# Mixer: the second rotation and the scan's input in PSUM in place of V, two scans of 264

## The chip, the cores and the metric

The kernel runs on one core of a Trainium2 chip. The metric is the device time of one execution in microseconds; lower is better. The core has five engines that run side by side and meet by semaphores: TensorE (PE, matrix products and transposes, its weight loads shown as PEld), VectorE (DVE), ScalarE (ACT), GpSimd (POOL) and SyncE (SP, which issues DMAs here). PE writes to PSUM, an accumulator memory of eight banks; DVE and ACT read and write both PSUM and SBUF, POOL works in SBUF alone.

## What is computed

A decoder trunk of two layers on 528 tokens (16 meta tokens and 512 of the input) with 1024 channels, all in float32. Layer 0 mixes tokens with a diagonal state-space model (S5), layer 1 with differential attention; each is followed by a gated conv-FFN. The change lies in the S5 mixer:

```python
def s5_mixer(u, a_re, a_im, log_dt, b_re, b_im, c_re, c_im, d_skip, w_glu, b_glu):
    """u: (B, L, D). Groups of 16 channels drive a 64-dim complex diagonal state (MIMO)."""
    ...
    ug = u.astype(f32).reshape(bsz, L, S5_GROUPS, S5_GROUP)
    bu_re = jnp.einsum('blgc,gnc->blgn', ug, bb_re)
    bu_im = jnp.einsum('blgc,gnc->blgn', ug, bb_im)
    a_seq_re = jnp.broadcast_to(ab_re, (1, L, S5_GROUPS, S5_STATE))
    a_seq_im = jnp.broadcast_to(ab_im, (1, L, S5_GROUPS, S5_STATE))
    _, _, s_re, s_im = lax.associative_scan(
        _complex_linear_combine, (a_seq_re, a_seq_im, bu_re, bu_im), axis=1)
    y = (jnp.einsum('blgn,gcn->blgc', s_re, c_re.astype(f32))
         - jnp.einsum('blgn,gcn->blgc', s_im, c_im.astype(f32)))
    y = y.reshape(bsz, L, D_MODEL) + d_skip.astype(f32) * u.astype(f32)
    z = jax.nn.gelu(y).astype(u.dtype)
    h = z @ w_glu + b_glu
    val, gate = jnp.split(h, 2, axis=-1)
    return val * jax.nn.sigmoid(gate)
...
    for i in range(DEPTH):
        j = i // N_MIXERS
        hn = rms_norm(h, norm_mix_gain[i])
        if i % N_MIXERS == 0:
            mix = s5_mixer(hn, ...)
        else:
            mix = diff_attention(hn, ...)
        h = h + mix.astype(h.dtype)
        hn = rms_norm(h, norm_ffn_gain[i])
        h = h + conv_ffn(hn, ffn_w_up[i], ffn_conv_w[i], ffn_conv_b[i], ffn_w_down[i]).astype(h.dtype)
```

The state of a group is a complex recurrence s(t) = a s(t-1) + B u(t) along the tokens, for 64 groups of 64 states.

## The kernel before

**Stages.** A prologue computes powers of a and the tables; the S5 loop runs over eight blocks of 128 channels (CT = 8, b = 0 to 7); then come the GLU (16 units of weights), the FFN of layer 0, attention with its output projection, and the FFN of layer 1. From the GLU on, weights are loaded, split into a high and a low part by ACT and POOL, and multiplied by PE.

**The S5 loop.** The 528 tokens are taken as NK = 66 chunks of T = 8. Within a chunk the outputs come from a direct product (TT, Toeplitz), between chunks from a state that is carried 66 times. Per block there are eight groups (BG), so real and imaginary part of four pairs (BQ) times 66 chunks make 2 x 264 = 528 columns on 128 partitions. PE's `inject(b)` (L708) writes these injections, V, to PSUM banks 2 and 3. A complex recurrence with a fixed rotation is turned into a real one: DVE's `scan(b)` multiplies V by the tables T1 and T2 of cosines and sines (L1650, L1651: "rotations", to rt1 and rt2), combines the products into zin (L1654, L1655: "sums"), shifted by one chunk, and runs one `tensor_tensor_scan` over 528 columns with the decay R (L1657) into zst. R is zero at the first chunk of each row, which restarts the scan. `states(b)` turns the result back (L1662, L1663), sums it to Sst (L1668, L1669), and PE multiplies it with E.

**The order of the work.** All orders are written out by hand, one instruction stream for each engine, with semaphores between them. In turn b of its loop

- DVE does `scan(b)`, `states(b)`, then for the next block E (`output_product`, `output_powers`, L1578 and L1594) and the tables T (`rotation_products`, `rotation_sums`, L1624 to L1633), and `z_rest(b - 1)` (L1676), the low part of the GLU's input.
- PE does `inject(b)`, transposes of x (L650), of z (L746) and of the scaled input (L662), then `input_weights(b + 1)` (L673, L675: transposes of F1 and F2 into PSUM banks 2 and 3), `state_outputs(b)` (L727, after DVE's Sst), `direct_outputs(b)` (L735, after the DMAs of TT) and `kernel_products(b + 1)` (L692, L697, after E). In turn 7 it has six tiles of GLU unit 0 (L769) in place of the input weights.
- ACT copies between PSUM and SBUF: among others `weights_out` (L1230, WBT, from the transposes), the first power of F (`unscaled_weights`, L1191), `decay` (R, L1251), `gelu` (L1268), `mirror` (L1258, the other half of the tables), `kernel_out` (L1240).
- POOL computes F1 and F2 of the next block (`input_power`, L525), four multiplications. It starts when DVE has finished that block's tables (`t_set`) and PE the last transposes (`ft_ps`). After the last tables it splits the weights of GLU unit 0 (L301).
- SP issues the DMAs of the inputs and, after `kernel_out`, the sixteen of TT by halves of the loop; then the GLU's weights.

`input_weights(b + 1)` may write banks 2 and 3 when V has been read: it waits for `v_read`, which the two rotations raise. GLU unit 1, which uses the same banks, waits for the same semaphore (L759).

## Time and profile before

| | us |
|---|---|
| median of three runs | 1314.66 |
| lowest and highest | 1309.7, 1315.55 |
| the profiled execution, device time | 1313.71 |
| its span in the profile | 1311.9 |
| mean granted clock of PE in it | 0.984 of full |

The profile gives for each engine the time in which it was busy, the idle time before an instruction and what ended it, and the chain of waits: the work that ended last, followed back to what released it. Times in the rows are us from the start of the span. PE and PEld overlap. "1.00" and "0.50" are the two levels of PE's granted clock, 2.4 and 1.2 GHz; a stretch that has both shows a mean between them.

### The profile page before, as it was taken

Reading aid. Unit: us, or ns where it says so; the run is one execution under the profiler, and the core shown is the slowest. Engines: PE = TensorE matmul, PEld = TensorE weight load, DVE = VectorE, ACT = ScalarE, POOL = GpSimd, SP = SyncE. Lnnn points to the kernel's source line nnn. Section 1 sums busy time; section 2 is a strip of 40 time slices with the busy share of each in tenths; the row PEclk is TensorE's granted clock in tenths of the full one; section 3 lists DMA queues with packets and bytes.
Section 4 is the critical chain, followed back from the end, with each engine's and each line's share of the span. In section 5 each row is a group of like instructions: output and inputs, shape, how many; then the busy total and the mean of one; then the engine's idle time right before and its main releaser. Section 6 shows DMA issues by size and latency. Waiting matters only on the chain.

```text
span 1311.9 us, 26207 instructions
## 1 busy us (share of the span) xinstructions
PE 1252.9 (96%) x10291; PEld 1192.5 (91%) x10291; DVE 764.3 (58%) x1027; ACT 566.0 (43%) x951; POOL 603.1 (46%) x365
## 2 busy tenths in 40 slices
PE   4787999999999999999999999989999999999998
PEld 4676899999999999999988889979999999997886
DVE  6699522388888886111345555553488888882002
ACT  6867443433334343222556665633334343432113
POOL 5223376543444435665644545407644444344441
PEclk9689999999999999999999999999999999999999
DMA  9222342233332232333221211212332323332221
GB/s 168 48 61 51 88 113 85 66 91 96 96 96 80 82 94 88 101 88 108 69 79 49 64 51 49 65 32 66 97 96 85 93 79 95 96 96 96 97 94 67
DMA packets 179546, 108.88 MB, mean 83 GB/s; under 512 B 7164, under 2 KB 173837, under 8 KB 179213
## 3 DMA queue, kind: packets, MB, share of 16 engines
q1 hardware_dynamic: 178885, 107.29, 29.2%
q8 instruction: 51, 0.84, 0.3%
q10 hardware_dynamic: 592, 0.60, 0.2%
q14 instruction: 18, 0.15, 0.0%
HBM read 101.58 MB, written 2.10 MB: 79 GB/s over the span
## 4 chain that ended last, share of the span: by engine, by line
PE 35%; issue 31%; DVE 14%; POOL 14%; ACT 4%; DMA 1%; DVEq 1%; POOLq 0%; ACTq 0%; SPq 0%
PE ps L877 9%; POOL wL L301 9%; PE ps L926 9%; PE ps L769 7%; DVE cv L1735 4%; DVE cv L1741 2%; PE ps L963 2%; PE ps L1033 1%; POOL acc L1960 1%; POOL sqt L1959 1%; DVE cg L1748 1%; DVE u L1730 1%; DVE u L1731 1%; PE ps L314 1%; ACT actH L1348 1%
## 5 line engine op out<-in xcount | busy, mean ns | idle before, releaser
L301 POOL TENSOR_TENSOR wL<-raw,wH 128x1024 fp32r<-128x1024 f32 x182 | 445.2, 2457 | 556.8 <-ACT wH L297 540.6
L297 ACT ACTIVATE wH<-raw 128x1024 fp32r<-128x1024 f32 x182 | 186.4, 1048 | 238.8 <-PE ps L314 82.9
L314 PE MATMUL ps<-hgH,wH 128*128 128x264 f32 (+1 forms) x1408 | 285.5, 284 | 2.7 <-DVE hgL L1698 2.7
L314 PE MATMUL ps<-hgH,wL 128*128 128x264 f32 (+1 forms) x1408 | 285.3, 284 | 0.0
L314 PE MATMUL ps<-hgL,wH 128*128 128x264 f32 (+1 forms) x1408 | 285.1, 284 | 0.0
L314 PEld LDWEIGHTS ps<-hgH,wH 128*128 128x128 f32 x1408 | 218.9, 189 | 3.2 <-issue 3.0
L314 PEld LDWEIGHTS ps<-hgL,wH 128*128 128x128 f32 x1408 | 218.4, 189 | 0.0
L314 PEld LDWEIGHTS ps<-hgH,wL 128*128 128x128 f32 x1408 | 217.8, 189 | 0.0
L1346 ACT ACTIVATE cg<-cg 128x528 f32<-128x528 f32 (+1 forms) x44 | 28.2, 640 | 268.2 <-DVE cg L1741 268.2
L1735 DVE TENSOR_SCALAR cv<-u,PV 128x528 f32<-128x528 f32 (+1 forms) x44 | 111.3, 2529 | 0.0
L1741 DVE SCALAR_TENSOR_TENSOR cg<-u,PV,cg 128x528 f32<-128x528 f32 (+1 forms) x88 | 97.3, 1105 | 13.0 <-DVE cv L1735 6.7
L926 PE MATMUL ps<-hgH,wH 128*128 128x264 f32 x384 | 83.7, 299 | 0.0
L926 PE MATMUL ps<-hgH,wL 128*128 128x264 f32 x384 | 78.6, 286 | 0.0
L926 PE MATMUL ps<-hgL,wH 128*128 128x264 f32 x384 | 78.4, 286 | 0.0
L314 PE MATMUL ps<-actH,wH 128*128 128x264 f32 x352 | 71.2, 283 | 0.0
L314 PE MATMUL ps<-actH,wL 128*128 128x264 f32 x352 | 71.2, 283 | 0.0
L314 PE MATMUL ps<-actL,wH 128*128 128x264 f32 x352 | 71.2, 283 | 0.0
L1741 DVE SCALAR_TENSOR_TENSOR cv<-u,PV,cv 128x528 f32<-128x528 f32 (+1 forms) x88 | 66.2, 752 | 0.0
L1409 ACT ACTIVATE Pb<-ps,tiny 128x144 f32<-128x144 f32 (+4 forms) x66 | 34.7, 531 | 69.3 <-DVE tiny L1789 69.2
L1763 DVE TENSOR_TENSOR ytok<-ps,fgain 128x512 f32<-128x512 f32 x4 | 2.8, 692 | 105.8 <-ACT ysq L1365 105.8
L926 PEld LDWEIGHTS ps<-hgH,wH 128*128 128x128 f32 x384 | 59.8, 191 | 3.9 <-issue 3.8
L1735 DVE TENSOR_SCALAR cg<-u,PV 128x528 f32<-128x528 f32 (+1 forms) x44 | 55.7, 1267 | 8.5 <-DVE u L1731 8.5
(299 smaller groups left out, 2375.0 us busy)
## 6 DMA issues: line engine op xcount, KB each, us to landing
raw<-ffn_w_up SPq DMA_DIRECT2D x88, 512.0 KB, 3.8
raw<-ffn_w_down SPq DMA_DIRECT2D x38, 512.0 KB, 3.5
raw<-attn_w_qkv SPq DMA_DIRECT2D x24, 512.0 KB, 3.7
raw<-s_w_glu SPq DMA_DIRECT2D x16, 512.0 KB, 4.0
TT<-KD SPq DMA_DIRECT2D x64, 64.0 KB, 2.4
raw<-attn_w_o SPq DMA_DIRECT2D x8, 512.0 KB, 4.1
raw<-ffn_w_down SPq DMA_DIRECT2D x8, 384.0 KB, 3.4
xb<-x SPq DMA_DIRECT2D x8, 256.0 KB
```

The lines of the kernel that those rows point to most:

```text
L297: nc.scalar.activation(wH[:, slot, 0:nk], raw[:, slot % 2, 0:nk], ACT.Copy).then_inc(w_hi, 1)
L301: nc.gpsimd.tensor_tensor(wL[:, slot, 0:nk], raw[:, slot % 2, 0:nk], wH[:, slot, 0:nk].bitcast(F32), ALU.subtract).then_inc(w_lo, 1)
L314: mm = nc.tensor.matmul(ps[:, bank + b, 0:tw], w[:, slot, k, :], x[:, kt, t0:t0 + tw], start=first and k == 0 and s0, stop=last and k == n ...
L769: mm = nc.tensor.matmul(ps[:, bank + b, 0:tw], w[:, n % 4, k, :], x[:, k, t0:t0 + tw], start=k == 0 and s0, stop=k == 7 and s1)
L877: mm = nc.tensor.matmul(ps[:, 2 * t + c, :], x[:, kt, tok], w[:, n % 4, 4 * c:4 * c + 4], start=False, stop=last and w is ws[-1] and x is ...
L926: mm = nc.tensor.matmul(ps[:, unit_bank(n) + b, 0:tw], w[:, n % 4, k, :], x[:, k, t0:t0 + tw], start=k == 0 and s0, stop=k == 7 and s1)
L963: return nc.tensor.matmul(ps_row[:, base[c] + a:base[c] + b], q[half[c], q0:nk], k[half[c], a:b], start=True, stop=stop)
L1033: mm = nc.tensor.matmul(out_at(i), AT[:, t, :], values, start=t == 0, stop=t == n_tiles(i) - 1)
L1346: nc.scalar.activation(cg[:, t0:], cg[:, t0:], ACT.Silu).then_inc(silu_set[l], 1)
L1409: ins = nc.scalar.activation(Pb[:, c, 0:nk], score_row(i, c), ACT.Exp, bias=mn[:, c:c + 1], scale=-1.0, accum_out=esum[:, c:c + 1])
L1735: ins = V.tensor_scalar(c[k][:, t0:], u[:, k, 2 + t0:2 + L], col(i, CONV_W + (3 * l + 2) * 2 * FT + k * FT + q), col(i, CONV_B + l * 2 * F ...
L1741: ins = V.scalar_tensor_tensor(c[k][:, t0:], u[:, k, t0 + j:L + j], col(i, CONV_W + (3 * l + j) * 2 * FT + k * FT + q), c[k][:, t0:], ALU. ...
```

## The change

The second rotation is written back over V in PSUM (`cells`), over all 66 chunks and not 65. The two sums take one operand from rt1 and one from `cells` and write to `cells` again, so that the scan's input stands in banks 2 and 3 in place of V, with real and imaginary part exchanged and no shift by one chunk. The scan over 528 columns of zin becomes two over 264 that read PSUM, one for each bank; both write to zst as before. `states` then turns 65 chunks and puts them one chunk later into Sst, whose first column is set to zero once ahead of the loop (before, zin's was). The tile zin goes. `input_weights(b + 1)` and GLU unit 1 wait for the scans (`z_scanned`) where they waited for the rotations (`v_read`).

```diff
--- before.py
+++ after.py
@@ -338,7 +338,6 @@
         WBT = s5("WBT", [P, BG, P], 0)
         rt1 = s5("rt1", [P, BG, NK], 0)
         rt2 = s5("rt2", [P, BG, NK], 0)
-        zin = s5("zin", [P, BG, NK], 0)
         zst = s5("zst", [P, BG, NK], 0)
         Sst = s5("Sst", [P, BG, NK], 0)
         U = s5("U", [P, 2, BG, NK], 0)
@@ -667,7 +666,7 @@
                 pe.wait_ge(f_set, b + 1)
                 pe.wait_ge(f7_set, b + 1)
                 if b:
-                    pe.wait_ge(v_read, 2 * b)
+                    pe.wait_ge(z_scanned, b)
                 for g in range(BG):
                     o = ps[:, 2 + g // 4, (g % 4) * P:(g % 4 + 1) * P]
                     nc.tensor.matmul(o, F1[:, g].rearrange("p j c -> p (j c)"), ident, is_transpose=True,
@@ -756,7 +755,7 @@
                     if n == 0:
                         pe.wait_ge(k_copied, CT)
                     elif n == 1:
-                        pe.wait_ge(v_read, 2 * CT)
+                        pe.wait_ge(z_scanned, CT)
                     elif n < 4:
                         pe.wait_ge(z_lo, CT)
                     else:
@@ -1597,7 +1596,7 @@
             output_product(0)
             output_powers(0)
             dve.wait_ge(x_sqrt, 1)
-            V.memset(zin[:, :, 0:1], 0.0)
+            V.memset(Sst[:, :, 0:1], 0.0)
             V.reciprocal(ssq[:, 0], ssq[:, 2]).then_inc(xr_set, 1)
             dve.wait_ge(gd_out, 1)
             V.tensor_tensor(dd, ident[32:32 + GC, 32:32 + GC].unsqueeze(1).broadcast_to([GC, G, GC]),
@@ -1645,28 +1644,30 @@
                 dve.wait_ge(v_ps, b + 1)
                 dve.wait_ge(t_mirrored, b + 1)
                 dve.wait_ge(r_set, b + 1)
+                v = ps[:, 2:4, 0:4 * NK]
+                cells = v.rearrange("p r (q k) -> p r q k", q=BQ)
+                V.tensor_tensor(parts(rt1), turns(T1, b, 1, NK + 1), cells, ALU.mult).then_inc(v_read, 1)
+                V.tensor_tensor(cells, turns(T2, b, 1, NK + 1), cells, ALU.mult).then_inc(v_read, 1)
+                dve.wait_ge(v_read, 2 * b + 2)
+                V.tensor_tensor(cells[:, 1], parts(rt1)[:, 0], cells[:, 1], ALU.add)
+                link(V.tensor_tensor(cells[:, 0], parts(rt1)[:, 1], cells[:, 0], ALU.subtract))
+                halves = lambda t: t.rearrange("p (r q) k -> p r (q k)", r=2)
+                for r in range(2):
+                    ins = V.tensor_tensor_scan(halves(zst[:, :, :])[:, r], halves(R[:, b % 2])[:, r], v[:, r], 0.0,
+                                               ALU.mult, ALU.add)
+                ins.then_inc(z_scanned, 1)
+                dve.wait_ge(z_scanned, b + 1)
+
+            def states(b):
                 w = NK - 1
-                v = ps[:, 2:4, 0:4 * NK].rearrange("p r (q k) -> p r q k", q=BQ)[:, :, :, 0:w]
-                V.tensor_tensor(parts(rt1, 0, w), turns(T1, b, 1, NK), v, ALU.mult).then_inc(v_read, 1)
-                V.tensor_tensor(parts(rt2, 0, w), turns(T2, b, 1, NK), v, ALU.mult).then_inc(v_read, 1)
-                dve.wait_ge(v_read, 2 * b + 2)
-                z, x, y = parts(zin, 1, NK), parts(rt1, 0, w), parts(rt2, 0, w)
-                V.tensor_tensor(z[:, 0], x[:, 0], y[:, 1], ALU.add)
-                link(V.tensor_tensor(z[:, 1], x[:, 1], y[:, 0], ALU.subtract))
-                flat = lambda t: t.rearrange("p g k -> p (g k)")
-                V.tensor_tensor_scan(flat(zst[:, :, :]), flat(R[:, b % 2]), flat(zin[:, :, :]), 0.0,
-                                     ALU.mult, ALU.add).then_inc(z_scanned, 1)
-                dve.wait_ge(z_scanned, b + 1)
-
-            def states(b):
-                V.tensor_tensor(parts(rt1), turns(T1, b, 0, NK), parts(zst), ALU.mult)
-                V.tensor_tensor(parts(rt2), turns(T2, b, 0, NK), parts(zst), ALU.mult).then_inc(s_half, 1)
+                V.tensor_tensor(parts(rt1, 0, w), turns(T1, b, 1, NK), parts(zst, 0, w), ALU.mult)
+                V.tensor_tensor(parts(rt2, 0, w), turns(T2, b, 1, NK), parts(zst, 0, w), ALU.mult).then_inc(s_half, 1)
                 dve.wait_ge(s_half, b + 1)
                 if b:
                     dve.wait_ge(y_ps, b)
-                s, x, y = parts(Sst), parts(rt1), parts(rt2)
-                V.tensor_tensor(s[:, 0], x[:, 0], y[:, 1], ALU.subtract)
-                V.tensor_tensor(s[:, 1], x[:, 1], y[:, 0], ALU.add).then_inc(s_set, 1)
+                s, x, y = parts(Sst, 1, NK), parts(rt1, 0, w), parts(rt2, 0, w)
+                V.tensor_tensor(s[:, 0], x[:, 1], y[:, 0], ALU.subtract)
+                V.tensor_tensor(s[:, 1], x[:, 0], y[:, 1], ALU.add).then_inc(s_set, 1)
                 dve.wait_ge(s_set, b + 1)
 
             def z_rest(b):
```

## Rows read from the trace of the kernel before

**Rows 1.** The page, part 1: busy us, share of span, instructions.

```profile
PE 1252.9 (96%) x10291; PEld 1192.5 (91%) x10291; DVE 764.3 (58%) x1027; ACT 566.0 (43%) x951; POOL 603.1 (46%) x365
```

**Rows 2.** Busy us by stretch and engine, then clock, DMA share, GB/s.

```profile
85.00:99.00 14.00, 12.48 (x168) 11.39 (x168) 13.45 (x22) 9.10 (x26) 4.20 (x5) 0.76 0.30 60
...
154.00:240.00 86.00, 86.00 (x713) 86.00 (x712) 20.08 (x24) 37.34 (x40) 58.23 (x30) 1.00 0.35 99
```

**Rows 3.** Chain of waits, start of the GLU: start us, us, what.

```profile
139.22 2.38 POOL wL L301
...
141.69 6.01 PE ps L769 x36
```

**Rows 4.** Timeline of DVE, turn 6: start us, us, line, operation, [idle before].

```profile
126.46 0.68 DVE L1650 TENSOR_TENSOR rt<-T,ps 128x520 f32<-128x520 f32 x1
...
127.07 0.68 DVE L1651 TENSOR_TENSOR rt<-T,ps 128x520 f32<-128x520 f32 x1
...
127.78 0.79 DVE L1654 TENSOR_TENSOR zin<-rt,rt 128x260 f32<-128x260 f32 x1
...
128.49 1.21 DVE L1655 TENSOR_TENSOR zin<-rt,rt 128x260 f32<-128x260 f32 x1
...
129.73 1.26 DVE L1657 TENSOR_TENSOR_SCAN zst<-R,zin 128x528 f32<-128x528 f32 x1
...
131.03 0.71 DVE L1662 TENSOR_TENSOR rt<-T,zst 128x528 f32<-128x528 f32 x1
...
138.81 0.33 DVE L1633 TENSOR_TENSOR T<-T,tmpE 128x160 f32<-128x160 f32 x1
...
140.25 0.69 DVE L1650 TENSOR_TENSOR rt<-T,ps 128x520 f32<-128x520 f32 x1
```

**Rows 5.** Timeline of POOL and PE in the same turn.

```profile
127.29 2.12 POOL L525 TENSOR_TENSOR F<-P,Bsw 128x448 f32<-128x448 f32 x2
...
127.43 0.68 PE L662 MATMUL ps<-cst,xg 66*128 66x66 f32 x8
...
129.47 0.33 PE L673 MATMUL ps<-cst,F 128*128 128x128 f32 x1 [1.36 <-POOL F L525]
...
131.96 0.39 PE L675 MATMUL ps<-cst,F 128*128 128x128 f32 x2
...
133.22 1.97 PE L727 MATMUL ps<-E,Sst 64*66 64x128 f32 x32 [0.87 <-DVE Sst L1669]
...
137.41 0.66 PE L692 MATMUL ps<-E,Bst 64*16 64x128 f32 x32 [0.33 <-DVE E L1594]
...
138.21 1.15 PE L708 MATMUL ps<-U,WBT 128*64 128x66 f32 x32
```

**Rows 6.** The sums: ns min/median/max; then busy us, mean ns.

```profile
L1654 DVE TENSOR_TENSOR zin<-rt,rt x8: 428/607/794, 44.4 to 141.6; 128x260 f32<-128x260 f32 x8
...
L1655 DVE TENSOR_TENSOR zin<-rt,rt x8: 421/1207/1218, 44.8 to 141.9; 128x260 f32<-128x260 f32 x8
...
L1655 DVE TENSOR_TENSOR zin<-rt,rt 128x260 f32<-128x260 f32 x8 | 7.3, 915 | 0.0
```

**Rows 7.** Timeline of turns 2 and 3, the latter at half clock.

```profile
71.03 0.69 DVE L1650 TENSOR_TENSOR rt<-T,ps 128x520 f32<-128x520 f32 x1
...
84.87 0.69 DVE L1650 TENSOR_TENSOR rt<-T,ps 128x520 f32<-128x520 f32 x1
...
87.89 0.48 PE L673 MATMUL ps<-cst,F 128*128 128x128 f32 x1 [1.35 <-POOL F L525]
...
93.20 2.10 PE L727 MATMUL ps<-E,Sst 64*66 64x128 f32 x32
...
99.12 0.69 DVE L1650 TENSOR_TENSOR rt<-T,ps 128x520 f32<-128x520 f32 x1 [0.33 <-PE ps L708]
```

**Rows 8.** DVE by line and form, FFN: busy us, mean ns, idle us.

```profile
L1748 DVE TENSOR_TENSOR cg<-cg,cv 128x528 f32<-128x528 f32 x22 | 15.6, 709 | 2.7
...
L1731 DVE TENSOR_TENSOR u<-ps,rstd 128x528 f32<-128x528 f32 x22 | 15.3, 697 | 0.0
```

More of the change, by code:

```diff
@@ L1647, in scan @@
                 dve.wait_ge(r_set, b + 1)
[L1648 to L1651 removed]
+                v = ps[:, 2:4, 0:4 * NK]
+                cells = v.rearrange("p r (q k) -> p r q k", q=BQ)
+                V.tensor_tensor(parts(rt1), turns(T1, b, 1, NK + 1), cells, ALU.mult).then_inc(v_read, 1)
+                V.tensor_tensor(cells, turns(T2, b, 1, NK + 1), cells, ALU.mult).then_inc(v_read, 1)
                 dve.wait_ge(v_read, 2 * b + 2)
[L1653 to L1658 removed]
+                V.tensor_tensor(cells[:, 1], parts(rt1)[:, 0], cells[:, 1], ALU.add)
[5 more added lines that the diff above has]
+                ins.then_inc(z_scanned, 1)
                 dve.wait_ge(z_scanned, b + 1)
             def states(b):
[L1662 to L1663 removed]
+                w = NK - 1
+                V.tensor_tensor(parts(rt1, 0, w), turns(T1, b, 1, NK), parts(zst, 0, w), ALU.mult)
+                V.tensor_tensor(parts(rt2, 0, w), turns(T2, b, 1, NK), parts(zst, 0, w), ALU.mult).then_inc(s_half, 1)
                 dve.wait_ge(s_half, b + 1)
```

1 line of the change is left out of this document (removed).

## The prediction

> **What bounds the kernel now.** The profiled execution spans 1311.9 us and its device time is 1313.71 us, so 1.8 us lie outside the span; the median of the three runs shown is 1314.66 us, 0.95 us above it. I read the page first: PE is busy for 96% of the span [rows 1]. Then the busy time by stretch: from 154 to 240 us, in the GLU after the S5 part, PE works through all of 86.00 us at a granted clock of 1.00, whereas in 85 to 99 us, inside the S5 loop, the clock is 0.76 and DVE is at 13.45 of 14 us [rows 2]. The edit lies in the S5 loop alone, so the question is when that loop lets PE go. The chain of waits says it: PE's first GLU products start at 141.69 us, behind a POOL subtraction of weights that started at 139.22 [rows 3]. That subtraction waits for DVE's last table of rotations, L1633, at 138.81 + 0.33 = 139.14 [rows 4]. From there PE has work to the end, so each us by which L1633 of the last table comes earlier should be a us of the kernel; what the last block does on DVE after it is covered by six GLU tiles (6.01 us [rows 3]).
>
> Next the timeline of DVE in one turn of the loop (block 6). From one L1650 to the next it takes 140.25 - 126.46 = 13.79 us, with no gap to speak of between its instructions [rows 4]. PE in the same turn has time: it waits for POOL before the input weights of block 7 (129.47), for DVE's states (133.22) and for E (137.41), and has V ready at 138.21 + 1.15 = 139.36, 0.9 us before DVE comes for it [rows 5]. So the loop goes at DVE's pace, where the clock is full. One turn is different: block 3, where the input weights run at half clock. They start at 87.89 and the next PE work at 93.20; V of block 4 is late and DVE waits 0.33 us for it; 99.12 - 84.87 = 14.25 us [rows 7].
>
> **The change part by part.**
>
> *The two sums (L1654, L1655) take one operand from PSUM.* Each reads two SBUF tiles now. Their shortest takes are 428 and 421 ns [rows 6]. In block 6 they last 0.79 and 1.21 us [rows 4], while POOL multiplies F from 127.29 to 129.41 [rows 5]; The median of the eight L1654 is 607 ns, midway between 0.43 and 0.785, so four of them are disturbed; the eight L1655 are busy for 7.3 us, and 3 x 0.42 + 5 x 1.21 = 7.3, so five of those are [rows 6]. What such a disturbance adds is 0.785 - 0.428 = 0.36 and 1.208 - 0.421 = 0.79 us. The rotations L1650 and L1651, which have one operand in PSUM, run at 0.68 us beside the same POOL work [rows 4, 5]. I take it that an instruction with only one SBUF input isn't held up by POOL, so the new sums lose the whole of it: 0.36 + 0.79 = 1.15 us in blocks 2, 3, 5 and 6, 0.79 in block 4.
>
> *Writing into PSUM.* No DVE instruction of the trace writes there. Three would in each block: the second rotation and both sums (the scans write to SBUF). Lower bound: as from PSUM to SBUF, 697 ns against 709 ns for SBUF to SBUF at 528 elements [rows 8], -0.01 each. Upper bound: in place, with reading and writing on one bank, half the pace; between 260 elements (0.421) and 520 (0.687) lie 0.27 us, so the elements alone are 0.54 us of the rotation and 0.27 of each sum [rows 4, 6], and all of them doubled is +1.1 us a block. I take 0, nearest to the rows that have a PSUM operand, and keep 1.1 as a rival.
>
> *Two scans of 264 for one of 528.* The one lasts 1.26 us and the step after it starts 1.30 us behind it [rows 4]. Two that follow without a wait: a rotation of 0.68 lets the next start 0.61 behind it (127.07 against 126.46), so 0.07 is overlapped; of the 0.687 for 520 elements 0.15 is not the elements' (above), so a second start costs 0.15 - 0.07 = 0.08 us. Reading PSUM in place of SBUF costs a tensor operation nothing [rows 8]; no scan of the trace does it. If PSUM slowed the scan as it might a write in place, half of it again would be 0.6 us; if its start were cheaper, both together could be 0.05 below today's 1.26. I take +0.08, the row's own price of a second start. The rotations get eight elements more each and each sum four, the state part as many fewer; what is left I put at 0.01. The memset that moves from zin to Sst is the same work before the loop.
>
> So a DVE turn at full clock: 13.84 (block 2's turn, 84.87 - 71.03 [rows 7]) - 1.15 + 0.09 = 12.78 us.
>
> There is a rule that speaks against it. The row shows no surcharge for PSUM: 697 ns from PSUM, 709 from SBUF [rows 8]. The Trainium skill, page "VectorE: DVE Perf Modes", section on the TRN2 errata, has a fixed 120 cycles for an instruction that reads PSUM against 58 for SBUF, 0.065 us more at its 0.96 GHz. By that the two sums and two scans would cost 4 x 0.065 = 0.26 us more a block and the forecast below would be 1.6 us higher. The trace disagrees, and I go by the row.
>
> *Input weights wait for the scan (L670).* PE may write banks 2 and 3 only after both scans. Queued behind this wait on PE are the states' outputs, the direct outputs, the next kernel products and inject; ACT's copy of WBT waits for the transposes, and behind it in ACT's queue F's first power, decay and gelu; POOL's next F waits for them too, and through the kernel products SP's transfers into TT. Counted from the start D of L1650: now F comes from POOL at 129.41 - 126.46 = D + 2.95 and the transposes start at D + 3.01 [rows 4, 5]. After: rotations 1.32 (127.78 - 126.46), undisturbed sums 0.80, scans 1.30 + 0.08, so scanned at D + 3.50, transposes at D + 3.56, 0.55 later. They take 2.8 us (129.47 to 131.96 + 0.39, less the 0.1 by which a next group of products may start ahead of that end [rows 5]), so the outputs start at D + 6.36; DVE has the states at D + 5.6 (6.7 now), so PE is what is late there, by 0.7. But the states' outputs themselves are earlier than now (133.22 - 126.46 = D + 6.76). Then the outputs, 3.86 us (137.41 less its wait of 0.33, less 133.22 [rows 5]): D + 10.2; E is ready at D + 9.8 now that DVE is 1.1 earlier, kernel products and inject 1.95 (137.41 to 139.36): V at D + 12.2. DVE comes for it at D + 12.78. The wait is hidden with 0.6 us to spare, at full clock. POOL's F is asked for at D + 6.3 and DVE's table lets it go only at D + 11.6, so POOL loses nothing; ACT's gelu has 1.5 us between the outputs and the mirror of the table, where it has 2.1 now. The other wait that moves, that of GLU unit 1 (L759), is reached behind six tiles and the last outputs, at 141.69 + 6.01 + 3.8 = 151.5 us; the last scan ends at 140.25 + 3.5 = 143.8, so it costs nothing.
>
> At half clock the cover is gone. The transposes take 93.20 - 87.89 = 5.31 us, 2.5 more [rows 7], V comes at D + 14.7 and the turn is 14.75 rather than 12.78.
>
> *The sum.* Blocks 2 to 6 take 140.25 - 71.03 = 69.2 us now [rows 4, 7]. With one turn at half clock as now: 4 x 12.78 + 14.75 = 65.9. Block 1 has no disturbance to lose and pays 0.09. Together 65.9 + 0.1 - 69.2 = -3.2 us. On the profiled execution that is 1313.7 - 3.2 = 1310.5, on the median 1311.5; I say 1311.
>
> **The rivals.**
>
> *PE loses its clock more often, with the wait as the cause, the slower side.* PE now idles 1.3 us before the transposes (127.43 + 0.68 = 128.11 to 129.47) and would idle 1.9. For it: the one turn at half clock came after just such a rest [rows 7]. Against: four turns with the same rest kept it, and the rest before the outputs disappears. Price: n turns at half clock give 63.99 + 1.97 n us against 69.2, so from three on the change costs time. With all five, 73.8: +4.6, 1318.3 us. If PE kept half clock for the whole turn (transposes 5.3, outputs 7.7, kernel products and inject 3.9, from D + 3.56) a turn would end at D + 20.4, 6.6 more than now: +33, 1346 us. The opposite, no turn at half clock, is 1308.5.
>
> *In place at half pace in PSUM.* A turn is 13.88, the one at half clock 15.85, block 1 +1.2: 4 x 13.88 + 15.85 + 1.2 - 69.2 = +3.4 us, 1317. For it: nothing in the trace excludes it. Against: no DVE row with PSUM is slower than its SBUF twin.
>
> *The disturbance moves on instead of going away.* POOL is at F until D + 2.95 and the scans would begin at D + 2.15; if they, with R in SBUF, wait for POOL, 0.8 us come back: turns of 13.58, in all 4 x 13.58 + 15.55 + 0.1 - 69.2 = +0.8, 1314.5 us: the change doesn't do what it says.
>
> **How the numbers follow.** Forecast 0.50; no half-clock turn 0.15; clock lost in two or more turns but not throughout 0.12; throughout 0.04; half pace in PSUM 0.11; disturbance moves on 0.08. The kernel's runs lie 5.9 us apart (1309.7 to 1315.55), so 0.5%, 6.6 us, is about what a measurement can tell: faster is below 1308.1, slower above 1321.2. Faster: most of the tail of the case without half clock and a tenth of the forecast's, 0.12. Slower: the clock lost throughout, and tails of the two dear cases, 0.07. Same: 0.81. The range takes in all but the clock lost throughout and the outer tails: 1305.5 to 1318.5.
>
> **What would show it.** Right: the new sums near 0.42 us in every block, even beside POOL's F; the second rotation near 0.69; two scans of about 0.7; L1650 to L1650 near 12.8 us in turns at full clock; PE's transposes released by the scan at D + 3.56; V ready before DVE comes; the GLU's first product near 138.5. Wrong: a rotation of 1.2 us (half pace), scans over 1 us beside POOL, DVE idle before the first rotation in several turns with PE's input weights at 5.3 us (clock), or an earlier GLU start whose gain is gone by the end of the GLU.

## The result

The changed kernel takes 1318.62 us in the median of 12 runs (1316.88 to 1321.75), the kernel before 1314.19 in as many; the ratio is 1.0031, with a 95% interval of 1.0020 to 1.0041. So it is 4.4 us slower, by less than the 0.5% that the chances go by, and outside the range of 1305.5 to 1318.5 by a tenth of a microsecond. The forecast was 3 us faster.

The profiled execution of the changed kernel is at 1316.96 us with a span of 1315.1, 3.2 above that of before. The page's first part, beside [rows 1]:

```profile
PE 1260.1 (96%) x10291; PEld 1200.3 (91%) x10291; DVE 759.8 (58%) x1035; ACT 565.5 (43%) x951; POOL 601.8 (46%) x365
```

PE is busy 7.2 us longer with the same 10291 products: it did some of them at a slower clock. The instructions that the change touches did what was said of them. By line of the changed kernel, ns min/median/max (L1650 the rotation in place, L1652 and L1653 the sums, L1656 the two scans):

```profile
L1650 DVE TENSOR_TENSOR ps<-T,ps x8: 705/705/706, 43.5 to 139.4; 128x528 f32<-128x528 f32 x8
...
L1652 DVE TENSOR_TENSOR ps<-rt,ps x8: 436/436/438, 44.2 to 140.2; 128x264 f32<-128x264 f32 x8
...
L1653 DVE TENSOR_TENSOR ps<-rt,ps x8: 430/430/431, 44.5 to 140.5; 128x264 f32<-128x264 f32 x8
...
L1656 DVE TENSOR_TENSOR_SCAN zst<-R,ps x16: 677/690/703, 45.0 to 141.6; 128x264 f32<-128x264 f32 x16
```

Against [rows 6] no sum is held up by POOL any more, in any block, writing in place in PSUM costs nothing (0.705 us for 528 elements, and 0.690 for 520 to SBUF before), and a second scan costs what was put down for it. The turn of the loop is another matter. Turn 5 of the changed kernel in the timeline (start us, us, engine, line, [idle before it and what ended it]), first PE's transposes of u, the input weights' first and a later one, the states' outputs and inject, then DVE's next first rotation:

```profile
112.65 0.69 PE L661 MATMUL ps<-cst,xg 66*128 66x66 f32 x8
...
115.11 0.45 PE L672 MATMUL ps<-cst,F 128*128 128x128 f32 x1 [1.77 <-DVE zst L1656]
...
118.93 0.27 PE L672 MATMUL ps<-cst,F 128*128 128x128 f32 x1
...
119.35 1.97 PE L726 MATMUL ps<-E,Sst 64*66 64x128 f32 x32
...
123.94 1.15 PE L707 MATMUL ps<-U,WBT 128*64 128x66 f32 x32
...
125.14 0.70 DVE L1649 TENSOR_TENSOR rt<-T,ps 128x528 f32<-128x528 f32 x1 [0.83 <-PE ps L707]
```

The input weights are released by the scan (1.77 us of idle time, against 1.36 in [rows 5]) at D + 3.62 with D = 111.49, as worked out. But their first transposes last 0.45 us and only the last ones 0.27: most of them run at half clock, the group takes 4.24 us and not 2.8, and DVE waits 0.83 us for V. The turn is 125.14 - 111.49 = 13.65 us. Not one turn in five is like this but all: the first rotations start at 70.57, 84.20, 97.84, 111.49, 125.14 and 138.79, so turns 2 to 6 take (138.79 - 70.57) / 5 = 13.64 us where 12.78 was forecast and 13.84 was before. Turn 1, in which POOL disturbed nothing before, has become longer; the first rotation of block 1 before, then those of blocks 1 and 2 in the changed kernel:

```profile
58.34 0.70 DVE L1650 TENSOR_TENSOR rt<-T,ps 128x520 f32<-128x520 f32 x1 [3.71 <-PE ps L708]
```

```profile
56.97 0.70 DVE L1649 TENSOR_TENSOR rt<-T,ps 128x528 f32<-128x528 f32 x1 [2.54 <-PE ps L707]
...
70.57 0.70 DVE L1649 TENSOR_TENSOR rt<-T,ps 128x528 f32<-128x528 f32 x1 [0.78 <-PE ps L707]
```

It takes 13.60 us against 71.03 - 58.34 = 12.69, because its input weights run at half clock now and did not before. Turns 1 to 6 together take 81.82 us, against 81.91 before: of the 3.2 us forecast for them, 0.1 came.

Busy us by stretch and engine (PE, PEld, DVE, ACT, POOL), then the granted clock; first the kernel before, then the changed one, each in the loop, at the GLU's start, between FFN and attention, and at the end of attention:

```profile
56.00:140.00 84.00, 68.19 (x1140) 60.48 (x1138) 79.27 (x132) 58.70 (x155) 23.57 (x24) 0.96 0.27 52
...
140.00:160.00 20.00, 18.99 (x167) 18.60 (x168) 8.84 (x15) 8.28 (x13) 8.79 (x4) 0.91 0.46 112
...
640.00:680.00 40.00, 37.48 (x285) 33.86 (x284) 16.63 (x34) 21.72 (x48) 22.90 (x17) 0.96 0.23 66
...
860.00:910.00 50.00, 46.41 (x359) 43.86 (x356) 20.74 (x34) 15.46 (x32) 17.07 (x10) 0.97 0.15 43
```

```profile
56.00:140.00 84.00, 72.31 (x1094) 66.13 (x1090) 76.12 (x140) 58.61 (x157) 23.98 (x24) 0.88 0.27 52
...
140.00:160.00 20.00, 17.64 (x150) 17.07 (x151) 7.21 (x14) 6.61 (x10) 7.11 (x3) 0.91 0.47 114
...
640.00:680.00 40.00, 37.35 (x271) 33.04 (x271) 16.46 (x32) 21.61 (x43) 22.93 (x17) 0.91 0.19 54
...
860.00:910.00 50.00, 46.55 (x347) 43.83 (x346) 21.75 (x38) 16.51 (x37) 14.12 (x8) 0.93 0.11 33
```

The clock column holds the loss: 0.88 for 0.96 in the loop, where the products are the same. At the GLU's start both have 0.91, and further on the changed kernel has 0.91 for 0.96 and 0.93 for 0.97, in stretches whose code is the same.

Where the 3.2 us arise, by the start of the same product of PE in both profiles: first GLU product 140.06 against 141.69, 1.6 earlier; in the GLU behind its first two units 1.1 later; after 660 us 2.65 later, after 880 us 3.6, at the end 3.2. The 1.6 us at the first GLU product are hardly the change's: 1.4 of them are there already at the first rotation of block 1 (56.97 against 58.34), from turn 0, where the half clock fell otherwise in this execution. The entry into the GLU turned this head start into a loss, and two later places added to it. The entry, first ACT and then PE's transposes of z for the last block:

```profile
150.24 1.06 ACT L297 ACTIVATE wH<-raw 128x1024 fp32r<-128x1024 f32 x1 [9.21 <-DMA raw<-s_w_glu]
...
151.20 1.06 ACT L1267 ACTIVATE Z<-ps 66x512 f32<-66x512 f32 x2
...
152.31 1.14 PE L745 MATMUL ps<-cst,Z 66*128 66x66 f32 x8 [2.21 <-ACT Z L1267]
```

ACT stands 9.2 us at the split of the weights of GLU unit 2 (L297), whose transfer was issued at 144.81, behind the eight of TT, and took 5.34 us; gelu of block 7 is behind it in ACT's queue, and PE waits 2.21 us for gelu. Before, the transfer was issued 1.3 us later and the split began at the same time all the same, 4.20 us behind the issue and not 5.43:

```profile
150.33 1.06 ACT L297 ACTIVATE wH<-raw 128x1024 fp32r<-128x1024 f32 x1 [7.96 <-DMA raw<-s_w_glu]
```

PE had done its first GLU tiles partly at half clock there (0.65 us for two products in place of 0.41) and came to these transposes at 152.80, when gelu was through. So this stretch was dearer by 2.7 us in the changed kernel's profile. The landing doesn't stand still, however: it follows the end of the loop, with the eight of TT in between. In e5, whose loop ends earlier, the split begins at 145.93, and in e1 at 154.29; with this order of ACT's queue it lies 8.6 to 10.3 us behind the first GLU product in all nine profiles.

```profile
145.93 1.06 ACT L297 ACTIVATE wH<-raw 128x1024 fp32r<-128x1024 f32 x1 [9.36 <-DMA raw<-s_w_glu]
...
154.29 1.06 ACT L297 ACTIVATE wH<-raw 128x1024 fp32r<-128x1024 f32 x1 [9.13 <-DMA raw<-s_w_glu]
```

### The profile page after: what moved, and what is told of

Read it like the earlier page. It is cut to its first block, busy times and chain, and to the rows that moved or that the text cites. A ratio compares the mean times of both kernels' runs of the same rounds, so it can differ in the third digit from the quotient of the medians.

```text
span 1315.1 us, 26215 instructions
## 1 busy us (share of the span) xinstructions
PE 1260.1 (96%) x10291; PEld 1200.3 (91%) x10291; DVE 759.8 (58%) x1035; ACT 565.5 (43%) x951; POOL 601.8 (46%) x365
## 4 chain that ended last, share of the span: by engine, by line
PE 37%; issue 30%; DVE 13%; POOL 12%; ACT 4%; DMA 2%; DVEq 1%; SPq 0%; POOLq 0%; ACTq 0%
PE ps L876 9%; POOL wL L301 9%; PE ps L925 9%; PE ps L768 7%; DVE cv L1736 4%; DVE cv L1742 2%; PE ps L962 2%; PE ps L1032 1%; POOL acc L1961 1%; PE ps L674 1%; POOL sqt L1960 1%; DVE cg L1749 1%; DVE u L1731 1%; PE ps L314 1%; DVE u L1732 1%
## 5 line engine op out<-in xcount | busy, mean ns | idle before, releaser
L297 ACT ACTIVATE wH<-raw 128x1024 fp32r<-128x1024 f32 x182 | 186.4, 1048 | 241.7 <-PE ps L314 79.5
```

The source lines that it names most:

```text
L297: nc.scalar.activation(wH[:, slot, 0:nk], raw[:, slot % 2, 0:nk], ACT.Copy).then_inc(w_hi, 1)
```

## The experiments

The median of each stands beside that of the kernel before on the same chip. "Turn" is the mean of turns 2 to 6, from the starts of the first rotation. e5 and e8 rest on four executions each, e6 and e9 on six; the clocks and starts are those of one profiled execution each.

| kernel | turn, us | clock, 56 to 140 us | first GLU product | clock, 140 to 160 us | median | before beside it | ratio (95%) |
|---|---|---|---|---|---|---|---|
| before | 13.84 | 0.96 | 141.69 | 0.91 | 1314.19 | | |
| changed | 13.64 | 0.88 | 140.06 | 0.91 | 1318.62 | 1314.19 | 1.0031 (1.0020, 1.0041) |
| e1 wait alone | 14.23 | 0.86 | 144.17 | 0.95 | 1318.50 | 1314.56 | 1.0024 (1.0006, 1.0043) |
| e2 sums to SBUF | 13.19 | 0.92 | 138.92 | 0.91 | 1311.04 | 1314.56 | 0.9974 (0.9960, 0.9988) |
| e3 changed, small fill | 13.78 | 0.88 | 143.28 | 1.00 | 1313.51 | 1314.56 | 0.9988 (0.9978, 0.9997) |
| e4 changed, gelu first | 13.71 | 0.88 | 140.83 | 1.00 | 1311.15 | 1314.56 | 0.9977 (0.9967, 0.9986) |
| e5 changed, full fill | 12.74 | 1.00 | 135.85 | 1.00 | 1309.11 | 1315.55 | 0.9945 (0.9924, 0.9967) |
| e6 before, gelu first | 13.84 | 0.92 | 140.34 | 1.00 | 1310.95 | 1315.55 | 0.9976 (0.9951, 1.0000) |
| e7 wait by bank | 13.37 | 0.90 | 138.74 | 0.92 | 1311.55 | 1315.55 | 0.9969 (0.9953, 0.9984) |
| e8 by bank, gelu first | 12.99 | 0.92 | 136.89 | 0.99 | 1308.16 | 1315.55 | 0.9937 (0.9916, 0.9958) |
| e9 changed, full fill, gelu first | 12.74 | 1.00 | 136.59 | 1.00 | 1307.23 | 1314.92 | 0.9944 (0.9931, 0.9957) |
| e10 by bank, fill of two, gelu first | 12.86 | 1.00 | 136.35 | 1.00 | 1308.14 | 1314.92 | 0.9953 (0.9932, 0.9973) |
| e11 before, full fill, gelu first | 13.84 | 1.00 | 142.50 | 1.00 | 1312.94 | 1314.92 | 0.9989 (0.9979, 0.9999) |
| e12 changed, again | 13.82 | 0.88 | 142.36 | 0.91 | 1317.34 | 1314.36 | 1.0026 (1.0011, 1.0041) |
| e13 before, again | 13.83 | 0.90 | 140.25 | 0.91 | 1314.85 | 1314.36 | 1.0007 (0.9987, 1.0027) |

**e1: the wait alone.** On the kernel before, in input_weights:

```diff
-                    pe.wait_ge(v_read, 2 * b)
+                    pe.wait_ge(z_scanned, b)
```

> The kernel before with one edit: the input weights' transposes wait for the scan, not for the rotations; contention of the sums and POOL stays. Theory W (the longer rest of PE ahead of the transposes costs the clock): the transposes start at D + 4.6 us instead of D + 3.0, they run partly at half clock in most turns (4 us or more instead of 2.8), V is late, DVE idles ahead of the first rotation, turns of about 14.5 to 15 us against 13.84, first GLU product 3 to 5 us later than 141.7. Rival P (half clock comes from the shorter turn, not from the wait): DVE's turn is still 13.84 with 1.1 us less slack, so at full clock V at D + 13.3, turn 13.84, GLU start within 0.7 us of 141.7.

Its mean turn is 14.23 us and its time 3.9 us above before. The first transpose of the input weights of one turn, DVE's first rotation of the next, and that of block 7:

```profile
103.55 0.45 PE L673 MATMUL ps<-cst,F 128*128 128x128 f32 x1 [1.95 <-DVE zst L1657]
...
113.64 0.70 DVE L1650 TENSOR_TENSOR rt<-T,ps 128x520 f32<-128x520 f32 x1 [0.85 <-PE ps L708]
...
142.90 0.70 DVE L1650 TENSOR_TENSOR rt<-T,ps 128x520 f32<-128x520 f32 x1 [2.12 <-PE ps L708]
```

The transposes run at half clock in part in each turn (the first one takes 0.45 us here) and DVE waits for V in each. That is the half of theory W that says that the wait has a price. But turns 2 to 5 are 14.01, 14.00, 13.88 and 13.83 us, hardly longer than before, and the mean is that of one long turn, the sixth, of 15.43 us, where the transposes took 5.36. The four are shorter than expected for two reasons: the clock comes back within the transposes, and while DVE waits POOL gets on with F, so that the second sum is undisturbed in every block (0.416 us in the median, 0.424 at most) and the first takes 0.68 to 0.97 in blocks 2 to 6. So this run does not keep the contention as it was. Rival P is not refuted by these turns; against it stand turn 1, at half clock and 13.74 us in place of 12.69, the sixth, and a first GLU product 2.5 us later.

**e2: the contention alone.** On the kernel before, the second rotation in place and the sums from PSUM to zin, waited for by PE:

```diff
-                    pe.wait_ge(v_read, 2 * b)
+                    pe.wait_ge(v_read, 3 * b)
...
-                        pe.wait_ge(v_read, 2 * CT)
+                        pe.wait_ge(v_read, 3 * CT)
...
-                V.tensor_tensor(parts(rt2, 0, w), turns(T2, b, 1, NK), v, ALU.mult).then_inc(v_read, 1)
-                dve.wait_ge(v_read, 2 * b + 2)
-                z, x, y = parts(zin, 1, NK), parts(rt1, 0, w), parts(rt2, 0, w)
-                V.tensor_tensor(z[:, 0], x[:, 0], y[:, 1], ALU.add)
-                link(V.tensor_tensor(z[:, 1], x[:, 1], y[:, 0], ALU.subtract))
+                V.tensor_tensor(v, turns(T2, b, 1, NK), v, ALU.mult).then_inc(v_read, 1)
+                dve.wait_ge(v_read, 3 * b + 2)
+                z, x = parts(zin, 1, NK), parts(rt1, 0, w)
+                V.tensor_tensor(z[:, 0], x[:, 0], v[:, 1], ALU.add)
+                V.tensor_tensor(z[:, 1], x[:, 1], v[:, 0], ALU.subtract).then_inc(v_read, 1)
+                dve.wait_ge(v_read, 3 * b + 3)
```

> The kernel before with the second rotation in place in PSUM and the sums reading it, but the sums write zin in SBUF and one scan of 528 reads it; the transposes wait for the sums (D + 2.15 us), which is before POOL has F (D + 2.95). So the contention goes and PE's rest ahead of the transposes stays at 1.3 us. Theory W: sums 0.43 us each, clock at full in most turns, turns of 12.7 us, first GLU product 4 to 5 us earlier than 141.7 (136.5 to 138). Rival P (a shorter turn by itself loses the clock): half clock in most turns and turns near 13.6 as in the changed kernel. In both, theory G says that little of it reaches the end: gelu of block 7 stands in ACT's queue behind the split of GLU unit 2, whose weights land near 150 us.

The turn is 13.19 us and not 12.7, and the half clock is still there (0.92). The half microsecond is DVE's own, in the scan over two SBUF operands, ns min/median/max:

```profile
L1658 DVE TENSOR_TENSOR_SCAN zst<-R,zin x8: 1256/1740/1770, 45.8 to 139.6; 128x528 f32<-128x528 f32 x8
```

Undisturbed it takes 1.26 us as in [rows 4], in most blocks 1.74: the sums are through before POOL is, and the scan now meets POOL's F in their place. The prediction had this as a rival for the scans that read PSUM. The changed kernel's own profile can't tell, since POOL is through with F before its scans begin (D + 1.90 against D + 2.17, as DVE comes 0.8 us late); in e5 and e9 the first scan runs 0.6 us beside POOL's F, and there no scan takes over 0.704 us. It is 3.5 us faster than before all the same.

**e3: PE kept busy with small products.** On the changed kernel, ahead of the input weights; the eight transposes of u are done three times, with the same result:

```diff
-                for g in range(BG):
+                for g in tuple(range(BG)) * (3 if b else 1):
```

> The changed kernel, PE does the eight transposes of the scaled input (u) three times over in turns 1 to 7, same operands and same place: 1.4 us of work into the rest of 1.9 us ahead of the input weights. Theory W: half clock gone from most turns, transposes 2.8 us, turns of 12.8 us, L1632 of the last table 4 us earlier than in the changed kernel (132.5 against 136.7). Rival (the scans' wait costs by its delay alone, not through the clock): turns stay at 13.65 or grow.

**e5: PE kept busy with products of the full array.** On the changed kernel, in the same place; what they write is written over by the transposes of u:

```diff
+                for k in range(3 if b else 0):
+                    nc.tensor.matmul(ps[:, 4, 0:264], ident, cst[:, 0:264], start=True, stop=True)
```

> The changed kernel; ahead of the eight transposes of the scaled input PE does three products of the full array (128 x 128 weights, 264 columns, identity and constants, to a place that the transposes then write over), some 1.3 us in the rest ahead of the input weights. Theory W' (the clock falls because PE does too little full work between inject and the input weights; the small transposes of the first filled kernel did not count): half clock gone from most turns, transposes 2.8 us, turns of 12.8 us. Rival (any turn in which PE waits for the scan loses the clock, whatever stands ahead of it): turns of 13.6 to 13.8 as before it.

The two belong together. The fill and the first transposes behind it in one turn, then the loop by stretch, first e3 and then e5:

```profile
101.93 1.69 PE L661 MATMUL ps<-cst,xg 66*128 66x66 f32 x24
...
104.38 0.45 PE L672 MATMUL ps<-cst,F 128*128 128x128 f32 x1 [0.77 <-DVE zst L1656]
...
56.00:140.00 84.00, 78.95 (x1165) 72.81 (x1162) 73.70 (x137) 58.64 (x150) 21.33 (x24) 0.88 0.27 52
```

```profile
97.24 1.57 PE L661 MATMUL ps<-cst 128*128 128x264 f32 x6
...
99.83 0.30 PE L674 MATMUL ps<-cst,F 128*128 128x128 f32 x1 [0.51 <-DVE zst L1658]
...
56.00:140.00 84.00, 77.90 (x1215) 69.52 (x1215) 79.81 (x148) 61.72 (x159) 23.84 (x24) 1.00 0.29 56
```

In e3 PE does 24 transposes of 66 x 66 for 1.69 us ahead of the rest, which shrinks from 1.77 to 0.77 us, and it is busy for 78.95 of 84 us; the first transpose lasts 0.45 us, the clock is 0.88 and the turn 13.78. In e5 it does six passes over 128 x 128 weights for 1.57 us and is busy for 77.90 us, no more; the clock is 1.00 and the turn is 12.74. So the expectation of e3 was a miss: its rest is shorter and the half clock is in every turn still, while behind the fill of e5 it is in none. A longer rest is not what separates them. E3 tells something else besides: it reaches the GLU 3 us later than the changed kernel (2.3 of them from turn 0) and is 5 us faster, with the clock at 1.00 instead of 0.91 at the GLU's start, so the end of the loop is not what makes the changed kernel the slower one. In e5, with the clock kept, the wait for the scan costs nothing: the transposes still start at 99.83 - 96.22 = D + 3.61 (96.22 being the start of the first rotation), and DVE never waits for V.

**e7: the wait taken apart by bank.** On the changed kernel:

```diff
-                if b:
-                    pe.wait_ge(z_scanned, b)
...
+                    if b and g % 4 == 0:
+                        pe.wait_ge(z_scanned, 2 * b + g // 4 - 1)
...
-                        pe.wait_ge(z_scanned, CT)
+                        pe.wait_ge(z_scanned, 2 * CT)
...
-                    act.wait_ge(z_scanned, b - 1)
+                    act.wait_ge(z_scanned, 2 * b - 2)
...
-                                               ALU.mult, ALU.add)
-                ins.then_inc(z_scanned, 1)
-                dve.wait_ge(z_scanned, b + 1)
+                                               ALU.mult, ALU.add).then_inc(z_scanned, 1)
+                dve.wait_ge(z_scanned, 2 * b + 2)
```

> The changed kernel with the wait by bank: the first four of the eight input weights (bank 2) wait for the first scan alone (D + 2.9), the other four (bank 3) for the second (D + 3.5). POOL has F at D + 2.95, so the transposes start at D + 3.0 as before the change. Theory W (the longer rest costs the clock): half clock in fewer turns, turns of 12.8 us where the clock holds, GLU start 2 us or more earlier than in the changed kernel (140.1). Theory P (the sparse work of the whole stretch, not the 0.6 us, loses the clock): half clock in most turns still, turns of 13.2 to 13.65.

The transposes start at D + 3.02 in every turn, and the turns are 12.76, 14.22, 12.75, 14.40 and 12.72 us: where the clock holds DVE sets 12.7 to 12.8, where it goes the input weights run at half clock as a whole. The mean, 13.37, is 0.27 below the changed kernel's, and the time is 4 us below before. The rest is now as short as before the change, and half clock still comes in two turns of five, so the rest of 0.6 us more is not needed for it. That it makes the half clock more frequent is another question, taken up at e12 and e13. The first GLU product, at 138.74, is 1.3 us earlier than in the changed kernel, not 2.

**e4 and e6: gelu ahead of the split.** One edit, in ACT's queue, made on the changed kernel (e4) and on the one before (e6):

```diff
                     decay(b + 1)
                 if b in (1, 2):
                     split_hi(act, b - 1, b - 1, 0)
+                gelu(b)
                 if b == CT - 1:
                     act.wait_ge(ft_ps, CT)
                     split_hi(act, 2, 2, 1)
-                gelu(b)
                 if b + 1 < CT:
                     mirror(b + 1)
                     kernel_out(b + 1)
```

> The changed kernel; in ACT's queue the gelu of block 7 comes ahead of the split of GLU unit 2 instead of behind it. Theory G (the gain at the GLU's start is lost where gelu waits behind a split whose weights land at 150.2 us): gelu at about 148.5 us instead of 151.2, PE's rest of 2.2 us ahead of the last transposes of z goes, PE is through the GLU's first two units 2 to 3 us earlier, whole time 2 to 4 us less than the changed kernel (about 1315). Rival (the weights of unit 2 themselves are what PE waits for next): the rest moves to unit 2 and the time stays at 1318.6.

> The kernel before with the gelu of block 7 ahead of the split of GLU unit 2 in ACT's queue. Theory G: there PE comes to the last transposes of z at 152.8 and gelu ends at 152.6, so the order costs nothing before the change: the time stays within 1 us of 1314.5. Rival (the order costs in both kernels, and the gain of the edit has nothing to do with the change): 2 us or more faster.

PE's transposes of z for the last block in e4, in e6, and in e13, which is the kernel before in another execution; then 140 to 160 us in e4 and e13:

```profile
150.71 0.66 PE L745 MATMUL ps<-cst,Z 66*128 66x66 f32 x8
...
150.05 0.66 PE L746 MATMUL ps<-cst,Z 66*128 66x66 f32 x8
...
152.43 1.14 PE L746 MATMUL ps<-cst,Z 66*128 66x66 f32 x8 [2.35 <-ACT Z L1268]
```

```profile
140.00:160.00 20.00, 19.20 (x180) 18.70 (x178) 8.12 (x15) 7.09 (x11) 7.15 (x3) 1.00 0.50 128
...
140.00:160.00 20.00, 17.39 (x150) 16.90 (x151) 7.19 (x13) 6.51 (x10) 7.28 (x4) 0.91 0.46 113
```

In e4 the wait for gelu is gone, and so is the half clock that follows it, just where PE is in the full work of the GLU: by the start of the same product e4 is 0.8 us later than the changed kernel at the first GLU product and 3.2 earlier behind the first two units. The ratio to the kernel before goes from 1.0031 to 0.9977, 7 us, more than expected; of the profiles' difference of 5.7 us the other 2.5 lie in the later stretches. E6 was a miss: by its ratio the edit gives 3 us before the change as well. E13 shows why. There the kernel before reached the GLU at 140.25 and not at 141.69; it waited 2.35 us for gelu and ran at 0.91 behind it, quite like the changed kernel. E6, which reaches the GLU at the same 140.34, has no such wait. So the order of the split and gelu costs time in either kernel, and more in the changed one. With gelu first the two stand side by side, 0.9977 (e4) and 0.9976 (e6): there the change is worth nothing, and it costs nothing.

How dear the entry is can be read from the first GLU product to the 200th record of PE behind it. It takes 25.9 to 26.2 us in the changed kernel, e12, e13, e1 and e2, where PE waits 2.1 to 2.4 us for gelu and half clock follows; 23.3 in before, 23.2 in e3, 24.4 in e5, 23.4 in e7; 21.9 to 22.4 in e4, e6, e9 and e11, with gelu first, and 23.5 in e8 and e10, gelu first too. Between e1 and e2, with the same entry, the first GLU product is 5.25 us apart and the 200th record 5.19; between e9 and e11 5.91 and 5.96. So an earlier end of the loop is passed on in full where the entry costs the same. The wait doesn't come from an early end: e12 and e1 end latest of the five and have it too.

**e8 to e11: both mends.** e8 is e7 with gelu first; e9 is e5 with gelu first; e10 is e8 with two products of the full array as fill; e11 is the kernel before with three and gelu first.

> Both edits, the wait by bank and gelu of block 7 ahead of the split of unit 2. If theories W and G both hold it is the fastest: 1308 to 1310 us. If the clock is lost all the same it is at 1311, like the changed kernel with gelu first (1311.15).

> The changed kernel with the three full-array products of e5 and gelu of block 7 ahead of the split of unit 2: both places where the change lost its gain are mended. Turns of 12.74 us, GLU start 135.9, PE through the GLU's first units without a wait for gelu. If the two theories add, 2 to 3 us less than e5 (1309.1): 1306 to 1307 us. If something else bounds the GLU's start (the landing of the weights of unit 2, at about 150 us with the DMAs of TT ahead of it), 1308 to 1309.

> Both mends and the wait by bank, with two full-array products in place of three. The transposes start at D + 3.0 and the clock should hold; DVE sets the turn at 12.74 us either way, so no gain over e9: within 0.5 us of it, if two products are enough for the clock; if they are not, half clock in some turns and 1308 (as e8).

> The kernel before with the same two mends (three full-array products, gelu first), without the change. Turns 13.84 us at full clock. What stands between it and e9 is the worth of the change where neither the clock nor the GLU's entry takes it: 5 x 1.1 + 0.8 less, so e9 should be 5 to 6 us faster if the prediction's sum for DVE (13.84 to 12.78 a turn) is right, and nearly level if it is not DVE that sets the turn there. Rival (the mends themselves are what makes e9 fast): this kernel is at 1306 to 1308 too.

The loop in e9 and in e11, by stretch:

```profile
56.00:140.00 84.00, 78.11 (x1215) 69.42 (x1214) 79.12 (x146) 61.96 (x160) 23.88 (x24) 1.00 0.29 56
...
56.00:140.00 84.00, 74.78 (x1183) 65.73 (x1181) 78.79 (x131) 59.35 (x153) 22.34 (x23) 1.00 0.27 52
```

Both have the clock at 1.00, the turns are 12.74 and 13.84 us, and the medians 1307.23 and 1312.94 us: 5.7 us for the change, where 5 to 6 was expected from DVE's sum. By the profiles turns 1 to 6 are 76.48 and 81.93 us, so 5.45 of it lie in the loop. The fill and gelu first alone bring the kernel before 1.4 us by the ratio, less than the 3 us of gelu first alone in e6, though the two intervals overlap. E8, e9 and e10, at 1307.2 to 1308.2, are the fastest kernels of the study, 0.5 to 0.6% below the one before, and their intervals overlap; e8 does it without a product that nobody reads. E10 adds nothing to e9, as expected, though it is 0.9 us slower where 0.5 was allowed. One expectation isn't borne out: gelu first was to bring 2 to 3 us over e5. The entry is 2.05 us shorter in e9's profile, but the ratios are 0.9945 and 0.9944, so the runs don't show that the two mends add.

**e12 and e13: both kernels once more.** No edit.

> The changed kernel once more, for a second profile. Theory L (the turns of the loop settle into step with the clock and so fix where the later half-clock stretches fall): half clock in every turn again, turns of 13.6 to 13.7, GLU start 139.5 to 141, half clock again near 152, more than one stretch near 660 or 880. Rival (chance): half clock in every turn, but the later stretches elsewhere or fewer, time between 1311 and 1319 accordingly.

> The kernel before once more, for a second profile. If one turn at half clock in five was typical: 1 turn at half clock or 2, GLU start 141 to 143. If the profile of before was a lucky one: half clock in three turns or more, GLU start still below 142.5, since DVE sets the turn.

The loop and the end of attention, first e12, then e13:

```profile
56.00:140.00 84.00, 72.93 (x1109) 66.51 (x1109) 74.76 (x138) 57.33 (x151) 22.62 (x24) 0.88 0.27 52
...
860.00:910.00 50.00, 46.23 (x341) 42.95 (x341) 22.07 (x40) 17.12 (x40) 13.71 (x8) 0.93 0.12 36
...
56.00:140.00 84.00, 72.81 (x1094) 65.68 (x1090) 80.98 (x134) 59.39 (x157) 24.68 (x24) 0.90 0.27 52
...
860.00:910.00 50.00, 46.23 (x316) 42.78 (x316) 21.37 (x36) 14.95 (x35) 10.78 (x7) 0.86 0.10 32
```

The kernel before had half clock in its input weights in each of turns 2 to 6 this time (their groups take 4.3 to 4.45 us up to the states' outputs, which without it come 3.75 behind), and its turn is 13.83 us all the same. The changed kernel has it in every turn again, and its turn is 13.82. E13's profiled execution is not a typical one: of 92 fast executions of the kernel before with a clock on record, 7 have a mean of 0.977 to 0.979 and take 1319.8 to 1320.7 us, and it is one of them; the median clock of the 92 is 0.985. But e6, whose loop is that of the kernel before and whose mean clock is 0.985, has the half clock in four of turns 2 to 6. So one in five, in the first profile, was few.

Over all profiles, turns 1 to 6, a group of transposes takes 2.8 to 2.9 us at full clock and 4.2 or more with half clock in it:

| kernels | turns with half clock |
|---|---|
| the first transposes may start before both scans are done: before, e13, e6, e2, e7, e8 | 20 of 36 |
| all transposes wait for the whole scan, with no fill or the small one: changed, e12, e4, e1, e3 | 30 of 30 |
| fill of the full array: e5, e9, e10, e11 | 0 of 24 |

In turn 1 the three profiles of the old loop (before, e13, e6) keep the clock and take 12.7 us; changed, e12, e4 and e1 lose it and take 13.6 to 13.8. The turns of one profile are not independent of each other, but the wait for the scans does go with a half clock in every turn, where the old wait had it in some.

The later stretches are not fixed: the clock at 860 to 910 us is 0.97, 0.93, 0.93 and 0.86 in the four profiles of the two kernels, and e13's execution took 1320.12 us, 5.3 above its median. Theory L has a clock of 0.91 at the GLU's start on its side again, but the turn of 13.82 us and a first GLU product at 142.36 were outside what it gave, and where the last stretches fall is not told by the kernel.

## Why the prediction was wrong

*What bounds the kernel now.* "Each us by which L1633 of the last table comes earlier should be a us of the kernel" took the entry into the GLU as a fixed length. Where it is one, the rule holds: e9 against e11, e1 against e2. But it varies from 21.9 to 26.2 us with PE's wait for gelu and the half clock, and it was 2.7 us longer in the changed kernel's profile than in that of before. The chain of waits named POOL's split of unit 0 as what releases the first GLU product, and I stopped there. The next wait behind it, gelu behind ACT's split of unit 2 (L297 at 150.24), cost 2.2 us of PE in the changed kernel and 2.35 in e13, and nothing where gelu is first. "What is late next" was asked of the loop and not of its exit.

*The change part by part.* DVE's sum was right in every term: sums 0.436 and 0.430 us in all blocks, nothing for writing to PSUM, 1.30 us for two scans, transposes at D + 3.6. The turn at full clock is 12.74 us in e5, e9 and in the good turns of e7, for 12.78 forecast; turns 1 to 6 are 5.45 us shorter in e9 than in e11, for 5 x 1.1 - 0.1. The surcharge for PSUM that the Trainium skill's page "VectorE: DVE Perf Modes" has in the cycle table of its section on the TRN2 errata (120 cycles against 58, by an estimate from its 0.96 GHz 0.065 us an instruction) appears in none of these rows.

*The wait.* "The wait is hidden with 0.6 us to spare, at full clock" holds (e5: DVE never waits). The step of the prediction that failed is the count behind it: one turn of five at half clock, "as now", taken from one profile, and none in turn 1. The runs showed it in all six turns of the changed kernel, in both its profiles, and turns 1 to 6 take 81.82 and 82.95 us, against 81.91 and 81.87 before, where 3.2 us less was forecast. E13 shows the kernel before with half clock in all of turns 2 to 6, e6 in four. It cost the kernel before nothing there. A half clock through part of the transposes makes 4.3 to 4.45 us of their 2.8, and the kernel before had two rests for the 1.6 us: PE waited 0.87 us for DVE's states, and V was 0.9 us ahead of DVE [rows 5]. Of these the change left 0.6 us in all, by my own account of it. In turn 5 of the changed kernel the transposes took 4.24 us, 1.46 more than in e5, and DVE waited 0.83 for V: that is the 1.46 less the 0.6. What I took for a rare event was a frequent one that the old turn covered, and the new wait goes with it in every turn. So in the changed kernel PE sets the turn, at 13.64 or 13.82 us, and the 1.1 us a turn that DVE gained is gone but for 0.0 to 0.2; turn 1, which had no disturbance to lose, is 0.9 to 1.1 us longer.

*The slower-side rival* had the mechanism by its name and, with all five turns, 1318.3 us; the measured 1318.6 is near it by luck, for a reason that is only in part the same: of its 4.6 us more in the loop the profiles have none in one pair and 1.1 in the other. Its price of a turn, 14.75 us, was too high (13.64 and 13.82, as the clock comes back during the transposes; only e7's turns of 14.22 and 14.40 and e1's of 15.43 come near). Its cause, the wait, has part of the truth: with it the half clock is in every turn, and e1 with the wait alone is 3.9 us above before, though most of what its turns 2 to 6 lose is in one of them. But the longer rest isn't the whole of it: e13 and e7 lose the clock with the short rest too, and e3 loses it with 0.77 us of rest. What it gave too much in the loop, the GLU's entry and later stretches added. I gave 0.12 to the clock in two or more turns; that was the case that came.

*The other rivals* are out: half pace in place (0.705 us for the rotation), and the disturbance that moves on (e5 and e9), which only e2 shows, for a scan with both operands in SBUF.

**Open.** The changed kernel's loop is level with before in one pair of profiles and 1.1 us slower in the other, and still it is 3 to 4.4 us slower. Its profile has 2.1 us of that at 660 and 880 us, in code that is the same, and e12 and e13 show such stretches move from one execution to the next in both kernels. What every execution shows is more half clock: the mean clock of the changed kernel is 0.975 to 0.981 in all 22, and that of the kernel before 0.985 in the median, at 0.981 or below in 13 of 92. At like clocks the changed kernel is no slower (its first twelve executions 1316.9 to 1321.8 us at 0.976 to 0.980; 1319.8 to 1320.7 before, at 0.977 to 0.979; one execution of before has 0.969 and 1314.12). That e4 and e6 are level points to the entry with gelu behind the split for what it loses outside the loop, but how often the kernel before has the dear entry, and why the full array's products keep the clock and the small transposes don't, isn't shown. A fill smaller than e10's two products was not run.

## What to carry to other kernels

Before taking slack from the engine that a wait leans on, look at more than one execution for what that slack absorbs: here it was a half clock that the first profile had in one turn of five, and two others in four and five. When a stage gets shorter, follow the queues past its end as well; here a gelu queued behind the wait for a transfer let PE stand for 2.2 us and run at half clock behind it, in either kernel, and moving it ahead was worth 7 us in the changed kernel and 3 in the one before, though nothing that the ratios show on top of e5. A DVE instruction whose second operand stands in PSUM isn't held up by POOL, and it can be written in place: worth 1.1 us of a 13.8 us turn, once the clock is kept.

## What the runs showed of the hardware

- The granted clock of PE fell to 1.2 GHz in each turn of e3, where PE did 1.69 us of 66 x 66 transposes ahead of the input weights (78.95 of 84 us busy, mean clock 0.88), and stayed at 2.4 GHz from 56 us to the end of the loop in e5, where it did 1.57 us of 128 x 128 products in their place (77.90 us busy, 1.00).
- A scan of 528 columns over two SBUF operands takes 1.74 us beside POOL's multiplications and 1.26 without (e2); two scans of 264 with one operand in PSUM take 1.30 us, in e5 and e9 with 0.6 us of it beside the same work. The port rule of the Trainium skill's page "SBUF — State Buffer", section "Who interferes with whom", has it so for instructions with two SBUF inputs against one, and these rows agree, the scan included.
- In place in PSUM, over two banks, 528 elements take 0.705 us, as from SBUF to SBUF (0.709 in [rows 8]).
